# Feed-forward sums by an all-ones matrix, and three re-ordered slab streams, in a two-block model kernel

## The reference

```python
xn = rms_norm_2(h, mix_pre_g[l]); proj = xn @ w_in[l]      # z, xbc, dt, q, k, v
y_ssd = ssd_mixer(z, xbc, dt_raw, ...)      # depthwise conv, scan over 5 chunks of 128, gate silu(z), norm
y_sb = rms_norm_2(stick_breaking_attention(q, k, v), sb_norm_g[l])      # 16 heads of 64
mix = concat([y_ssd, y_sb]) @ w_out[l]
h = h + rms_norm_2(mix, mix_post_g[l])
xn = rms_norm_2(h, ffn_pre_g[l]); gu = xn @ w_up[l]      # 2 x 2816 columns
g = causal_dwconv(gu[..., :D_FF], ffn_conv_w[l], ffn_conv_b[l])
f = (gelu(g) * gu[..., D_FF:]) @ w_down[l]
h = h + rms_norm_2(f, ffn_post_g[l])
```

## Time and profile before

| | us |
|---|---|
| median of 3 runs (lowest, highest) | 1780.92 (1778.61, 1782.13) |
| the profiled execution's own time | 1780.02 |
| its span, first to last instruction | 1778.2 |
| PE busy | 1638.7 (92%) |
| DVE busy | 1006.8 (57%) |
| POOL busy | 909.0 (51%) |
| ACT busy | 492.4 (28%) |
| mean granted clock | 0.955 |

### The profile page before, as it was taken

The page is one execution under the profiler, slowest core; times in us unless marked ns, Lnnn a source line. Parts: engine busy times, 40 slices in busy tenths (PEclk is TensorE's granted clock), DMA queues, the critical chain, the costliest instruction groups (busy, mean ns, idle before and its releaser), DMA issues.

```text
span 1778.2 us, 29250 instructions
## 1 busy us (share of the span) xinstructions
PE 1638.7 (92%) x10712; PEld 1403.6 (79%) x10712; DVE 1006.8 (57%) x1500; ACT 492.4 (28%) x1041; POOL 909.0 (51%) x838
## 2 busy tenths in 40 slices
PE   5799998978999999897898999999998999999997
PEld 3687865865888887797887887888897899998885
DVE  3877315237545885685876887776334366666001
ACT  3201012112115673222223555554213111111011
POOL 0454420334575343475535764444371477777774
PEclk9899999987999999898999999999995799999999
DMA  7354420113320001232111111111221133233332
GB/s 273 123 196 156 144 59 0 36 35 107 95 83 13 2 25 36 59 83 71 36 35 49 48 48 37 49 46 48 60 84 36 48 94 91 87 93 103 92 95 88
DMA packets 208527, 131.86 MB, mean 74 GB/s; under 512 B 5262, under 2 KB 194222, under 8 KB 208318
## 3 DMA queue, kind: packets, MB, share of 16 engines
q1 hardware_dynamic: 208446, 130.74, 24.3%
HBM read 128.63 MB, written 2.10 MB: 74 GB/s over the span
## 4 chain that ended last, share of the span: by engine, by line
PE 80%; DVE 12%; ACT 3%; issue 2%; DMA 1%; POOL 0%; SPq 0%; DVEq 0%; ACTq 0%; POOLq 0%
PE ps L2026 20%; PE ps L2027 19%; PE ps L2029 19%; PE ps L2291 2%; PE ps L2317 2%; PE ps L2585 2%; DVE sb_sum L1853 1%; PE ps L2213 1%; PE ps L2495 1%; PE ps L2278 1%; DVE seg L1773 1%; PE ps L2269 1%; PE ps L2560 1%; DVE op_lo L1334 1%; PE ps L2647 1%
## 5 line engine op out<-in xcount | busy, mean ns | idle before, releaser
L701 POOL TENSOR_SCALAR w_hi<-raw 128x512 fp32r<-128x512 f32 x370 | 287.2, 776 | 764.3 <-PE ps L2029 375.9
L703 POOL TENSOR_TENSOR w_lo<-raw,w_hi 128x512 fp32r<-128x512 f32 x370 | 529.0, 1430 | 30.9
L2026 PE MATMUL ps<-op_hi,w_hi 128*128 128x512 f32 x704 | 256.0, 364 | 23.2 <-DVE op_lo L1334 15.0
L2026 PE MATMUL ps<-xn_hi,w_hi 128*128 128x264 f32 (+1 forms) x848 | 247.4, 312 | 12.2 <-ACT zs L1067 3.1
L2027 PE MATMUL ps<-op_lo,w_hi 128*128 128x512 f32 x704 | 242.3, 360 | 0.0
L2027 PE MATMUL ps<-xn_lo,w_hi 128*128 128x264 f32 (+1 forms) x848 | 225.6, 286 | 0.0
L2029 PE MATMUL ps<-op_hi,w_lo 128*128 128x512 f32 x704 | 211.1, 359 | 0.0
L2026 PEld LDWEIGHTS ps<-op_hi,w_hi 128*128 128x128 f32 x704 | 134.9, 192 | 65.4 <-DVE op_lo L1334 12.9
L2026 PEld LDWEIGHTS ps<-xn_hi,w_hi 128*128 128x128 f32 x848 | 161.6, 191 | 27.7 <-issue 15.2
L2026 PE MATMUL ps<-u_hi,w_hi 128*128 128x258 f32 (+1 forms) x528 | 167.4, 330 | 7.6 <-DVE u_lo L1913 5.4
L2029 PE MATMUL ps<-xn_hi,w_lo 128*128 128x264 f32 (+1 forms) x848 | 173.1, 286 | 0.0
(11 more groups left out here) (379 smaller groups left out, 2944.5 us busy)
## 6 DMA issues: line engine op xcount, KB each, us to landing
raw<-in_w_in SPq DMA_DIRECT2D x45, 512.0 KB, 3.8
raw<-in_w_up SPq DMA_DIRECT2D x44, 512.0 KB, 3.8
ada_ring<-in_ada_w SPq DMA_DIRECT2D x16, 1024.0 KB, 6.0
raw<-in_w_in_ab SPq DMA_DIRECT2D x20, 512.0 KB, 3.8
raw<-in_w_in_c SPq DMA_DIRECT2D x20, 512.0 KB, 3.8
ada_first<-in_ada_w SPq DMA_DIRECT2D x4, 2048.0 KB, 19.9
raw<-in_w_out SPq DMA_DIRECT2D x16, 512.0 KB, 4.0
raw<-in_w_down SPq DMA_DIRECT2D x16, 512.0 KB, 3.9
```

Of the source, the lines that this page charges most:

```text
L701: steps(nc.gpsimd.tensor_scalar(hi, r, 1.0, 0.0, ALU.mult, ALU.add))
L703: nc.gpsimd.tensor_tensor(lo, r, hi.bitcast(F32), ALU.subtract)\
L2026: mm(o[:, 512 * b:512 * b + n], w_h[:, k, :], hi[:, k0 + k, c0:c0 + n], start=a, stop=False)
```

## The change

It has four parts. (1) `ffn_sums` streams the squares against a 128 x 128 matrix of ones, in two matmuls of 388 and 128 columns, and so leaves the sums in every partition of `FFN_SUMS`; ACT takes the root of the 516 columns, DVE the reciprocal in place; the spreading matmuls and the copy go. The sums of block k come after the transposes of block k+1, the transposes all use one bank, and ACT makes u_hi two blocks ahead. (2) SP loads four query slabs ahead of its wait instead of two. (3) The first z slab is multiplied before the scan, all later slabs of the scan move up by one place, and the half value slab behind the scan goes; ACT's copies follow. (4) POOL waits, before it splits slab g with g >= 3 and g % 3 == 0 (the queries of the next pair), for the subtraction behind the first long sum of the current pair.

```diff
-        def x_tok_ps(k):
-            return bank(7) if k % 2 == 0 else gemm_ps[(BLOCK0["up"] + 1) % 2][:, 512:1024]
+        X_TOK_PS = gemm_ps[(BLOCK0["up"] + 1) % 2][:, 512:1024]
+        FFN_SUMS = pair_ps[1][:, PAD + CUT:TP]
...
-            stream("q", plain(w_in_c, 0), 0, 1)
+            stream("q", plain(w_in_c, 0), 0, 2)
             sp.wait_ge(s["op_ready"], OP_DONE["l1"])
...
-            stream("q", plain(w_in_c, 0), 1)
+            stream("q", plain(w_in_c, 0), 2)
...
             for g in range(-2, 24):
+                if g >= 3 and g % 3 == 0:
+                    pool.wait_ge(s["sb_d"], len(SBU) * (g // 3 - 1) + 8)
                 slab((g0 + 3 + g) // 2, (g0 + 3 + g) % 2, True)
...
                     if g == 0 and more:
                         chunk_in(i, j + 1)
+                    elif g == 0:
+                        act.wait_ge(s["ssd_used"], NT)
+                        clear_other(0)
+                        take(0, 0, g0 + 1)
                 if more:
-                    take_z(2 * i + j, 0)
-                else:
-                    act.wait_ge(s["ssd_used"], NT)
-                    clear_other(0)
-                    take(0, 0, g0 + 1)
+                    take_z(2 * (2 * i + j) + 1)
...
-                if more:
-                    take_z(2 * i + j, 1)
-                else:
+                if more and 2 * i + j < NT - 2:
+                    take_z(2 * (2 * i + j) + 2)
+                elif not more:
                     take(0, 1, g0 + 2)
...
-            with act.Fori(0, NT // 2) as i:
-                for j in range(2):
-                    chunk(i, j, True)
-            chunk(NT // 2, 0, False)
+            take_z(0)
+            for t in range(NT):
+                chunk(t // 2, t % 2, t < NT - 1)
...
+            ffn_hi(0)
+            ffn_hi(1)
+            for k in range(KC):
+                if k + 2 < KC:
+                    ffn_hi(k + 2)
                 act.wait_ge(s["sq_used"], 8 * k0 + max(k - 1, 0))
                 nc.scalar.activation(sq3[:, k % 2, CUT:T2], xT[:, k, CUT:T2], ACT.Square).then_inc(s["sq"], 1)
                 if k:
                     take_x_tok(k - 1)
             take_x_tok(KC - 1)
-            norm_std("ffn")
+            act.wait_ge(s["ssq"], k0 + 1)
+            nc.scalar.activation(rstd_ffn[:, CUT:T2], FFN_SUMS, ACT.Sqrt, bias=eps[:, 0:1], scale=1.0 / D)\
+              .then_inc(s["std"], 1)
...
-            norm_rstd("ffn")
-            steps(nc.vector.tensor_copy(rstd_ffn[:, CUT:T2], rstd_rows("ffn", CUT, T3)))
+            dve.wait_ge(s["std"], NORMS["ffn"][0] + 1)
+            steps(nc.vector.reciprocal(rstd_ffn[:, CUT:T2], rstd_ffn[:, CUT:T2]))
...
+            z_chunks(0, 0, 0, KC)
...
-                        if g > -3:
-                            pe.wait_ge(s["sb_evac"], 3 + g)
-                        else:
-                            pe.wait_ge(s["z_evac"], KC + 1)
+                        pe.wait_ge(s["sb_evac"], 3 + g)
...
                     if more:
-                        z_chunks(t, 0, 4 * g, 4 * g + 4)
+                        z_chunks(t, 1, 4 * g, 4 * g + 4)
                     else:
-                        first_chunks(-3, 4 * g, 4 * g + 4)
+                        first_chunks(-2, 4 * g, 4 * g + 4)
                 if not more:
-                    first_chunks(-2, 0, KC)
+                    first_chunks(-1, 0, KC)
                 else:
-                    z_chunks(t, 1, 0, KC)
+                    z_chunks(t, 2, 0, KC)
...
-            first_chunks(-1, 0, KC // 2)
...
-                if k >= 2:
-                    pe.wait_ge(s["x_tok_taken"], k - 1)
+                if k:
+                    pe.wait_ge(s["x_tok_taken"], k)
...
-                for t, (c0, n) in enumerate(tiles):
-                    ins = mm(o[0:n, t:t + 1], sq[:, k % 2, c0:c0 + n], ones[:, 0:1], start=False, stop=True,
-                             skip_group_check=True)
+                split_at = 512 - PAD - CUT
+                for c0, c1 in ((0, split_at), (split_at, T3)):
+                    ins = mm(FFN_SUMS[:, c0:c1], ones[:, :], sq[:, k % 2, CUT + c0:CUT + c1], start=(k == 0),
+                             stop=(k == KC - 1))
                 ins.then_inc(s["sq_used"], 1)
...
             def beside_up(k):
                 turn_x_tok(k)
-                ffn_sums(k)
+                if k:
+                    ffn_sums(k - 1)
+                if k == KC - 1:
+                    ffn_sums(k)
...
-            gemm("up", u_hi, u_lo, SEG_3, ready=OP_DONE["sbn"], beside=lambda: sums_rows("ffn"), odd_segs=SEG_LAT,
-                 each=beside_up)
+            gemm("up", u_hi, u_lo, SEG_3, ready=OP_DONE["sbn"], odd_segs=SEG_LAT, each=beside_up)
```

More of the change, by code:

```diff
@@ L1063, in _, with take_z @@
             g0z = SLAB0["z"]
[L1065 to L1068, removed]
+            def take_z(n):
+                act.wait_ge(s["slab_done"], g0z + n + 1)
+                nc.scalar.copy(two(zs[:, n, PAD:TP]), halves(gemm_ps[0])).then_inc(s["z_evac"], 1)
             g0 = SLAB0["sb"]
@@ L1230, in take_x_tok, with ffn_hi @@
                 act.wait_ge(s["x_tok_turned"], k + 1)
-                nc.scalar.copy(x_tok[:, :, k * P:(k + 1) * P], tok4(x_tok_ps(k))).then_inc(s["x_tok_taken"], 1)
-            for k in range(KC):
+                nc.scalar.copy(x_tok[:, :, k * P:(k + 1) * P], tok4(X_TOK_PS)).then_inc(s["x_tok_taken"], 1)
+            def ffn_hi(k):
                 act.wait_ge(s["norm_done"], 8 + k + 1)
@@ L2526, in sb_iteration @@
             def sb_iteration(i, last):
-                chunk = -4
+                first = isinstance(i, int) and i == 0
+                chunk = 0 if first else -4
                 for u in range(sb_steps(last)):
                     chunks = SB_CHUNKS.get(u, 0) if u <= len(SBU) or not last else 0
+                    if first and u == 0:
+                        chunks = 0
                     tail = last and u in MIX_TAIL
@@ L2630, in turn_x_tok @@
             def turn_x_tok(k):
-                if k >= 2:
-                    pe.wait_ge(s["x_tok_taken"], k - 1)
+                if k:
+                    pe.wait_ge(s["x_tok_taken"], k)
                 for t in range(S // P):
-                    ins = nc.tensor.transpose(x_tok_ps(k)[:, t * P:(t + 1) * P],
+                    ins = nc.tensor.transpose(X_TOK_PS[:, t * P:(t + 1) * P],
                                               xT[:, k, META + t * P:META + (t + 1) * P], ident[:, :])
@@ L2639, in ffn_sums @@
             def ffn_sums(k):
-                k0, tiles, _, sq, _ = NORMS["ffn"]
-                o = pair_ps[1]
-                if k == 0:
-                    mm(o[:, 0:NT], zeros[:, :], zeros[:, 0:NT], start=True, stop=True)
+                k0, _, _, sq, _ = NORMS["ffn"]
                 pe.wait_ge(s["sq"], 8 * k0 + k + 1)
-                for t, (c0, n) in enumerate(tiles):
-                    ins = mm(o[0:n, t:t + 1], sq[:, k % 2, c0:c0 + n], ones[:, 0:1], start=False, stop=True,
-                             skip_group_check=True)
+                split_at = 512 - PAD - CUT
+                for c0, c1 in ((0, split_at), (split_at, T3)):
+                    ins = mm(FFN_SUMS[:, c0:c1], ones[:, :], sq[:, k % 2, CUT + c0:CUT + c1], start=(k == 0),
+                             stop=(k == KC - 1))
                 ins.then_inc(s["sq_used"], 1)
```

## The result

| | before | after |
|---|---|---|
| median of the runs (lowest, highest), us | 1780.65 (1778.61, 1782.13) | 1756.28 (1754.22, 1757.09) |
| profiled execution, us | 1780.02 | 1757.03 |
| its span, us; mean granted clock | 1778.2; 0.955 | 1755.2; 0.964 |
| PE busy, us | 1638.7 | 1622.2 |

The ratio is 0.986, with a 95% interval of 0.9846 to 0.9874: the changed kernel is 24.4 us faster by the medians. 1753.6 had been forecast, in a range of 1744 to 1767. The gain is 3 us smaller than forecast. Two of the four terms promised too much, Part 3 by 4 to 5 us and Part 4 by 1.4, and a stretch that stood in no term gave 3.2 us back. This shows only when the gain is followed through the kernel.

The account below looks back on a forecast made before the run. TensorE was taken to bound the kernel, where it idles, runs at its lower clock or waits for other engines. Terms -18.2 - 7.1 + 0.5 - 2.5 = -27.3 gave 1752.7 profiled, 1753.6 us median; range 1744 to 1767.

Parts of the forecast that it names:

- The reciprocal: Feed-forward tail beside slab two: 516 columns take 3.80 us, in proportion to 943 ns for 128 columns.
- the gain hangs on the clock: Feed-forward rounds: one-column records keep 1.2 GHz; with wide streams the clock rises about 5 us in, at round two's end.
- a chain over one bank: Feed-forward rounds at full clock: square, copy, semaphores, transposes and sums follow each other over X_TOK_PS, 2.75 us a round.
- The front: Ahead of the scan: the moved gate slab keeps PE busy, transposes may run at full clock; gain 1.2, between 0 and 4.
- The first wait: Scan's last chunk: the first slab waits for ACT's evacuation of the query slab, +2.3 us to the second exponential.
- The second wait: Scan's last chunk: the second slab waits for ACT's evacuation behind both gate exponentials; 4.6 us idle, +3.4 in all, low clock +2.
- The gain of 3.7: Behind the scan: with four chunks taken out, the stick-breaking stage's first transposes come 3.7 us earlier relative to the scan's end.
- the overlap: Stick-breaking pairs: the delayed POOL split of 4.0 us ends some 0.3 us into the next long scan.
- Rival 1: Feed-forward: the clock stays at 0.50 through the rounds, Part 1 gives -6, total 1766 us; chance 0.14.
- rival 4: Stick-breaking stage: POOL's delayed split holds DVE's next scan 4.1 us in seven pairs, +28.7, total 1785 us; chance 0.03.
- rival 2: Feed-forward clock falls back or rounds take 3.6, last chunk at its dear end, 1 us from part 4: 1763; chance 0.14.
- dear end: Scan's last chunk: the costly end of Part 3's forecast, +3.5 us, against +0.5 forecast.

Follow-up runs that it names:

- filler: The kernel before with one unused 128x512 fp32 matmul added in each feed-forward round, ahead of the transposes, old sums kept: 1775.12 us, 0.997.
- copy_first: The changed kernel with ACT's copy of the previous round's turned tokens put ahead of the square in the feed-forward rounds: 1752.30 us, 0.9844 of before.
- query_slabs_only: The kernel before with only the second part, four query slabs loaded ahead: 1771.12 us, 0.9947 of before.
- keys_early: The changed kernel with ACT taking the key slab ahead of the gate exponentials in the scan's last chunk: 1750.66 us, 0.985 of before.
- no_gate_move: The changed kernel with all edits of the third part taken back, first gate slab again in the scan's first chunk: 1753.22 us, 0.9843 of before.
- ff_sums_only: The kernel before with only the first part, the new feed-forward sums: 1761.04 us, 0.9887 of before.

## Why the prediction was right, and where its steps were not

**Part 1, forecast -18.2, measured -18.4 in the trace and -18.8 alone.** The clock rose at the end of round two, a round is 2.73 us (2.75), first product to third slab 29.5 (29.7), PE idle ahead of it 0 (0 to 0.5). The reciprocal took 3.38 us, not 3.80: the scaling from the earlier trace rows was 12% high, without effect, since slab two covers it. The reason given, that the gain hangs on the clock, is borne out by `filler`. What the prediction called a chain over one bank is right, but it took the order on ACT as given; `copy_first` shows 4 us there. That the total fits to 0.2 is in part luck: in four other kernels with the same rounds the clock rises a round earlier and the first product to third slab takes 28.0 to 28.2, near the -20 that the prediction gave as an end.

**Part 2, forecast -7.1, measured -7.1 at the value tokens.** Two windows of after, columns as in rows 2, show that PE runs through what had been 5.74 us of idle, at full clock from 422 on. By the last convolution block the lead has grown by 0.7, in `query_slabs_only` by 0.8; no term stood for that.

```profile
416.00:422.00 6.00, 6.00 (x21) 4.78 (x20) 0.00 (x1) 0.60 (x1) 3.79 (x4) 0.71 0.81 276
422.00:428.00 6.00, 6.00 (x28) 4.82 (x27) 3.97 (x5) 0.60 (x1) 3.47 (x4) 1.00 0.53 164
```

**Part 3, forecast +0.5 (ends -4.5 and +3.5), measured +4.3 to +5.9.** The step that failed is the granted clock behind the waits of the last chunk and behind the scan. The front was right: 1.5 against 1.2 (0.7 against the kernels without the move whose clock came back earlier there), the first transposes at full clock (1.09 us for 1.94), the cumulative sums at 0.50 (3.78 us, as before). The last chunk failed in its terms of the clock. The first wait was forecast at 2.3 and is 2.34, but the four chunks of slab behind it run at 0.50 (942.72 to 948.34, 5.6 us; 2.9 at full clock), which the sum left out: second exponential 5.2 late, not 2.3. The second wait is 4.59 (forecast 4.6 with +2 of low clock and +3.4 for the chunk). From the last exponential to the outputs' evacuation 3.0 more are lost. The gain of 3.7 at the stage's first transposes came (3.9), but the price of the same edit did not stand in the sum: with the half value slab gone, and with it the pieces in the stage's first unit, little keeps PE streaming between 969 and 975, the clock falls (0.56 in the window from 972), and from the first transposes to the first long sum 26.7 us pass instead of 23.7. The clock accounts for it: 23.7 in every kernel without the move, 25.0 in `keys_early` with 3.4 us of low clock there, 26.7 with 6.8. Sum: 5.2 + 3.0 - 3.9 + 3.0 - 1.5 = 5.8, against 5.9 from `no_gate_move`.

**Part 4, forecast -2.5, measured -1.1 in the stage and -1.3 by the medians.** The first long sum fell to 1.25 as forecast. The failed step is the overlap: the split was to end 0.3 us into the next long sum. With 4.0 us for the split that leaves 3.7 us ahead of the next sum. In before 3.7 is the distance from the end of the long sum itself (1068.89 + 2.30) to the next one (1074.91); the subtraction, for which POOL waits, ends 0.7 later, so 3.0 were there. Here the split runs from 1070.55 to 1074.49 and the second sum starts at 1073.69, so the distance is 3.1; the last 0.8 us of the split lie on the second sum, which grows from 1.25 to 1.91. PE then waits there: its waits for the sums' exponentials are 10.1 us in after and 10.3 without the wait, from 1000 to 1270.

**The part that was not in the sum.** The forecast treated 1270 to 1350 us as a fixed stretch. It is 2 to 4 us shorter where the clock does not fall at the thirty sums, and after happened to be such a case. Of the 4.3 that the lead grows from the first long sum to the feed-forward norm, 1.1 is Part 4's and 3.2 this. It hid more than half of Part 3's price, and that the total was right within 3 us is luck of this kind: errors of +5.3 in Part 3 and +1.4 in Part 4 stand against -3.2 from a term that was missing. Rival 1 did not occur, nor rival 4: no split came late. Of rival 2 the feed-forward half did not occur, since the round stayed at 2.73, but its two other conditions did: the last chunk came out beyond its dear end, and Part 4 gave about 1. Two readings in the prediction are off without effect: PE stopped ahead of the scan at 824.8, not 825.7, and the 0.6 us of idle that rival 2 names would make rounds of 3.35 us, not the 3.6 that it counts with.

## What to carry to other kernels

An evacuation that a matrix stream waits for costs twice, the wait and the clock behind it, so a slab moved into a new place needs its evacuation placed as well, ahead of whatever that engine would otherwise do first. Sums of one column each are cheap in number and dear in clock: stream the data against a matrix of ones, or put the columns between wide products. When a change moves a later stage in time, compare leads at several aligned events, in more than one trace, and not the medians alone, since a clock fall that one kernel meets and the other does not can hide a term of the same size.

## What the runs showed of the hardware

With PE busy all the time, the granted clock fell from 1.00 to 0.50 within thirty one-column records (`no_gate_move`: records from 1261.9 to 1266.1, clock down at 1264.4), in seven of ten traces at or just behind them, and rose from 0.50 to 1.00 in the second of eight rounds when one matmul of 512 columns was added to rounds that were otherwise the same. A reciprocal of 128 x 516 fp32 took 3.38 us, 6.6 ns a column, against 7.4 at 128 columns. Beside a POOL split a scan of 528 columns took up to 2.30 us, 1.25 alone. The Trainium skill (GPSIMD Engine Reference, Specifications) says that GpSimd's SBUF interfaces are shared with VectorE, with contention for "DVE instructions in a 2-port perf mode or with two SBUF inputs"; the scan has two such inputs, and this agrees. The first scaled block of the first norm came at 49.88 us in before and at 53.09 in `ff_sums_only`, with the same code ahead of it.
